# Forget-gate logits in strips over summed halves, and parameter arithmetic one block later, in a hybrid decoder layer

## The chip, the cores and the metric

The kernel runs on one core of a Trainium2 chip. The metric is device time in microseconds (us) from launch to end, as the median of several executions; lower is better. A core has a matrix engine (TensorE, "PE" in the profile, with its weight loads as "PEld"), three elementwise engines (VectorE or "DVE", ScalarE or "ACT", GpSimd or "POOL"), and SyncE ("SP"), which here only starts transfers. Each engine has its own instruction queue and runs it in order. Engines wait for each other on semaphores. SBUF is the on-chip memory; matrix products land in PSUM, in banks of 512 float32 columns.

## The reference

One layer with 256 tokens and model width 4096, everything in float32:

```
u = rmsnorm(h, g_pre);  p = u @ w_in          # 4096 x 12296
fq fk fv fgate f_logit sq sk sv sgate su ssm_gate lx lru_gate = split(p)
log_f  = log_sigmoid(f_logit + b_forget)      # 8 heads, one column of p each
o_fox  = softmax attention over fq, fk, fv, biased by the cumulative sums of log_f
o_sb   = stick-breaking attention over sq, sk, sv
o_ssm  = S5 state space over su: lam_bar = exp(lam*dt), b_bar = (lam_bar-1)/lam * b, scan, then GLU
o_lru  = gated linear recurrence over lx: log_a = 8 * r * log_sigmoid(lambda)
mixed  = concat(each o * silu(its gate)) @ w_out
out    = h + rmsnorm(mixed, g_post)
```

The `f_logit` part of the projection is only 8 columns wide. It stands for 4096 x 8 weights against the 256 tokens. `lam_bar`, `b_bar` and `log_sigmoid(lambda)` are small per-feature arrays that depend on parameters alone.

## The kernel before

**Blocks and chunks.** `w_in` (without the 8 forget columns) is cut into 24 blocks of 512 columns and `w_out` into 8. Blocks 0 to 3 give the sources `su` and `lx`, 4 to 11 queries and keys, 12 to 15 values, 16 to 23 the gates, 24 to 31 the output. A block is 16 chunks (`CH`), each of 2 x 128 rows of the contraction: 512 KB of weights. All chunks go through a ring of four buffers: SyncE loads `w_raw`, ScalarE writes the rounded half `w_hi` (`high`, line 620), VectorE the rest `w_lo` (`low`, line 1000), and TensorE does 12 matmuls of 512 columns (lines 303 to 305): for both groups of 128 tokens and both rows of the chunk u_hi*w_hi, u_hi*w_lo, u_lo*w_hi. `high` and `low` run `LEAD` = 3 chunks ahead of TensorE.

**The order of the work** is written out by hand. Each engine has a loop over the blocks with a loop over the chunks inside, and everything else is hung at a fixed chunk number: `if c == 4: ...`. Block 0 is written out. In it TensorE turns the 32 tiles of x (`turn`, line 354: two tiles, four transposes, in each chunk). ScalarE takes the turned tile as the high half of u (`take_high`, line 661) and VectorE the low half (`take_low`, line 1131), both into `acts[:, k, :]`: 256 columns of high half and 256 of low half. The matmuls of a chunk wait for the halves of their tiles (`u_lo`). ScalarE also squares x for the norm (`square_half`, line 655, in chunks 5, 7, 9 and 11), and the norm's root stands in chunks 12 to 14. After each block its result is turned by eight transposes (`turn_rows`, line 344) in chunk 1 of the next.

**Forget logits.** `wf` holds the 32 x 8 forget columns split in a high and a low part, padded to 128 columns of weights. From chunk 5 of block 0 on three matmuls in each chunk (line 379), 32 in all, multiply them with both halves of u at once, 512 columns, into `main[:, 2, :]`. ScalarE copies the cross part (line 708), VectorE adds it (line 1176), and TensorE waits for that (`fl_dve`) before the turn in block 1. In block 1 `token_logits` (line 388, chunk 3) adds high and low rows by a matmul that also turns the result so that tokens are rows, `forget_values` adds bias and norm, ScalarE and VectorE form the log-sigmoid, `forget_sums` (lines 395 to 397, chunk 9) the cumulative sums.

**Parameter arithmetic.** `s5_angles`, `s5_expm1` and `s5_factors` (10, 11 and 10 small VectorE instructions of 128x32) and `lru_series`, `lru_decays` stand in chunks 4, 9, 10, 5 and 7 of block 0, their exponentials, tangent and sines on ScalarE in chunks 2, 6 and 8. `take_s5(0)` (line 1181) then copies the first group's parameters, `take_source(0)` (line 1185) the first source behind block 3; `s5_inputs` (line 425) waits for the latter in chunk 0 of block 4. `s5_outputs` (line 436) are matmuls with 32-column weights, each into its own 32 partitions of PSUM.

**Loops.** Block 1 is written out; blocks 2 and 3 are the two passes of a loop on each of TensorE, ScalarE and VectorE. GpSimd makes constants at the start and has nothing else to do until block 4.

Of the kernel before, what the change touches and what calls it, by code (L numbers as in the profile page):

```python
# [6 lines left out]
F32 = mybir.dt.float32  # L7
# [6 lines left out]
P = 128  # L14
# [45 lines left out]
def hybrid_trunk(nc, x, par, bt, ct, wfg, wglu, wri, gpost, wall, out):  # L60
    ctx = ExitStack()
    with ctx:
        def sb(name, shape, dt=F32):
            return ctx.enter_context(nc.sbuf_tensor(name, shape, dt))
# [20 lines left out]
        small = sb("small", [P, 147])  # L85
        wf = sb("wf", [P, 2 * NK * FT + P], F32R)
        later = sb("later", [P, 2 * P])
# [21 lines left out]
        wf_raw = scr[:, 0:256].rearrange("p (k n) -> p k n", k=NK)  # L109
        wf_parts = wf[:, 0:2 * NK * FT].rearrange("p (k r n) -> p k r n", k=NK, r=2)  # L110
        fl_sel = small[0:2 * FT, 64:64 + FT]
        s5tmp = scr[:, 256:800].rearrange("p (n f) -> p n f", n=17)
# [6 lines left out]
        s5_y = main[:, 3, 0:T]  # L119
        logits = main[:, 2, :]  # L120
        rows = cross[:, :, :].rearrange("p j t -> p (j t)").rearrange("p (a n) -> p a n", a=TT)
# [35 lines left out]
        ss_base = small[:, 72:74]  # L157
        fl_cross, fl_rows = scr[:, 3584:3840], scr[:, 3840:4096]
        fl_z, fl_e = (small[:, 112 + 16 * n:128 + 16 * n].rearrange("p (a n) -> p a n", a=TT)
# [27 lines left out]
        pa, pd = sem("pa"), sem("pd")  # L187
        wf_hi, wf_lo0, wf_lo = sem("wf_hi"), sem("wf_lo0"), sem("wf_lo")
        fl_mm, fl_act, fl_dve = sem("fl_mm"), sem("fl_act"), sem("fl_dve")
# [28 lines left out]
        MIX_AT, MIX_LATE = (4, 5, 6, 7, 10, 11, 12, 13, 15), 3  # L218
        FL_AT = 5
        SPLIT = [2, 3, 4, 5] + [c + LEAD for c in range(4, CH + 1)]  # L220
# [68 lines left out]
        def _(pe):  # L289
# [78 lines left out]
            for c in range(CH):  # L368
                for k in range(max(KC * c + 2, 4), min(KC * c + 4, NK)):
                    turn(k)  # L370
                if c == 0:
                    first_chunk()
                else:
                    pe.wait_ge(u_lo, KC * (c + 1))
                    chunk_in(0, c)
                if c == FL_AT:
                    pe.wait_ge(wf_lo, 1)
                for k in range(3 * (c - FL_AT), min(3 * (c - FL_AT + 1), NK)) if c >= FL_AT else ():
                    mm = pe.matmul(logits, wf[:, 2 * k * FT:2 * k * FT + P], acts[:, k, :], start=(k == 0),  # L379
                                   stop=(k == NK - 1))  # L380
            mm.then_inc(fl_mm, 1)


            def src_block(i):
                def token_logits():

                    for a in range(TT):
                        mm = pe.matmul(side[:, 2, a * FT:(a + 1) * FT], fl_rows[0:2 * FT, a * P:(a + 1) * P],
                                       fl_sel, start=True, stop=True)
                    mm.then_inc(fl_mm, 1)  # L390

                def forget_sums():

                    pe.wait_ge(lf_ready, 1)
                    pe.matmul(side[0:FT, 1, 0:P], logf[:, 0, :], upto[:, :], start=True, stop=True)
                    pe.matmul(side[0:FT, 1, P:T], logf[:, 0, :], later[:, 0:P], start=True, stop=False)
                    pe.matmul(side[0:FT, 1, P:T], logf[:, 1, :], upto[:, :], start=False,
                              stop=True).then_inc(dec_mm, 1)

                for c in range(CH):  # L400
                    if c == T_AT:
                        if isinstance(i, int):
                            pe.wait_ge(fl_dve, 1)
                        turn_rows(i - 1, i - 1)
                    if c == 3 and isinstance(i, int):
                        token_logits()
                    if c == 9 and isinstance(i, int):
                        forget_sums()
                    chunk_in(i, c)

            src_block(1)
            with pe.Fori(2, B_QK - B_SRC) as i:
                src_block(i)
# [200 lines left out]
        def _(act):  # L614
# [62 lines left out]
            for c in range(CH):  # L677
                for k in range(max(KC * c + 2, 4), min(KC * c + 4, NK)):
                    take_high(k)
                for n in range(SPLIT[c], SPLIT[c + 1]):  # L680
                    high(0, n)
                if c == 2:
                    act.activation(tmp(0), col("log_dt"), ACT.Exp).then_inc(pa, 1)

                    act.activation(log_a[0], col("lam"), ACT.Abs).then_inc(pa, 1)
                    act.wait_ge(pa, 2)
                    act.activation(log_a[0], log_a[0], ACT.Exp, scale=-1.0).then_inc(pa, 1)
                if c == 3:
                    act.wait_ge(wf_in, 16)
                    act.activation(wf_parts[:, :, 0, :], wf_raw, ACT.Copy).then_inc(wf_hi, 1)  # L690
# [5 lines left out]
                if c == 6:  # L696
                    act.wait_ge(pd, 9)
                    act.activation(tmp(4), tmp(1), ACT.Exp).then_inc(pa, 1)
                    act.activation(tmp(5), tmp(1), ACT.Tanh, scale=0.5).then_inc(pa, 1)
                if c == 8:  # L700
                    act.activation(tmp(6), tmp(3), ACT.Sin, scale=TWO_PI).then_inc(pa, 1)
                    act.activation(tmp(7), tmp(3), ACT.Sin, scale=TWO_PI / 2).then_inc(pa, 1)
# [22 lines left out]

            act.wait_ge(wf_lo, 1)
            load_inputs(0)

            def src_block(i):
                for c in range(CH):  # L730
                    high(i, c + LEAD)
                    if c == T_AT + 1:
                        take_turned(i - 1)
                    if c == 5 and isinstance(i, int):
                        act.wait_ge(fl_dve, 3)
# [4 lines left out]
                        act.activation(fl_e, fl_e, ACT.Ln, bias=1.0).then_inc(fl_act, 1)  # L740
                    if c == 10 and isinstance(i, int):
                        act.wait_ge(dec_mm, 1)
# [5 lines left out]

            src_block(1)
            with act.Fori(2, B_QK - B_SRC) as i:  # L750
                src_block(i)
# [242 lines left out]
        def _(dve):  # L994
# [151 lines left out]
            for c in range(CH):  # L1146
                for k in range(max(KC * c + 2, 4), min(KC * c + 4, NK)):
                    take_low(k)
                for n in range(SPLIT[c], SPLIT[c + 1]):
                    low(0, n)  # L1150
                if c == 3:

                    dve.memset(wf[:, 2 * NK * FT:2 * NK * FT + P].bitcast(F32), 0.0).then_inc(wf_lo0, 1)
                    dve.wait_ge(wf_hi, 1)
                    dve.wait_ge(consts, N_CONST)
                    dve.tensor_tensor(fl_sel, ident[0:2 * FT, 0:FT], ident[0:2 * FT, FT:2 * FT],
                                      ALU.add).then_inc(wf_lo0, 1)
                    dve.wait_ge(wf_lo0, 1)
                    dve.tensor_tensor(wf_parts[:, :, 1, :], wf_raw, wf_parts[:, :, 0, :].bitcast(F32),
                                      ALU.subtract).then_inc(wf_lo, 1)  # L1160
                if c == 4:
                    s5_angles()
                if c == 5:
                    lru_series()
                if c == 7:
                    lru_decays()
                if c == 9:
                    s5_expm1()
                if c == 10:
                    s5_factors()  # L1170
# [4 lines left out]
            dve.wait_ge(fl_act, 1)  # L1175
            dve.tensor_tensor(fl_rows[0:2 * FT, :], logits[0:2 * FT, 0:T], fl_cross[0:2 * FT, :],
                              ALU.add).then_inc(fl_dve, 1)

            def take_s5(f):
# [6 lines left out]

            dve.wait_ge(pd, n_pd)
            take_s5(0)

# [15 lines left out]
            def src_block(i):  # L1205
                for c in range(CH):
                    low(i, c + LEAD)
                    if c == 4 and isinstance(i, int):
                        forget_values()
                    if c == 7 and isinstance(i, int):  # L1210
                        log_forgets()

            src_block(1)
            with dve.Fori(2, B_QK - B_SRC) as i:
                src_block(i)
            dve.wait_ge(t_free, FT // JB)
            take_source(0)
# [308 lines left out]
        def _(pool):  # L1526
# [175 lines left out]
```

## Time and profile before

| | |
|---|---|
| median of 3 executions | 1525.13 us (1524.93 to 1525.23) |
| profiled execution: from first to last instruction (span) | 1523.3 us |
| TensorE busy | 1513.9 us (99%) |
| VectorE, ScalarE, GpSimd busy | 940.3, 874.8, 102.7 us |
| granted TensorE clock | 0.999 of full speed |
| read from memory | 287.56 MB, 192 GB/s |

The span is one profiled execution's; the runs' times hold about 1.8 us around it. "Busy" adds up instructions of an engine, with overlaps counted once. The chain of work goes back from the last instruction to what released it each time. Times of a matmul in a list of groups overlap those of its neighbours, and the distance between starts is what one costs in a row. A f32 matmul is two records; one with a 32-column weight is written 128*32.

### The profile page before, as it was taken

What the parts mean: (1) busy time and instruction counts of PE and PEld (TensorE: products, weight loads), DVE (VectorE), ACT (ScalarE), POOL (GpSimd) and SP (SyncE); (2) the same over time, 40 slices, a digit from 0 to 9 for tenths busy, and PEclk for the clock granted to TensorE, in tenths of its full rate; (3) what the DMA queues carried; (4) which work ended last, traced back from release to release, by engine and by line L of the source; (5) the groups of instructions that cost most, each with busy time, mean ns of one, the idle gap of its engine ahead of it and who ended that gap; (6) DMA issues with size and microseconds to landing.
All of it is one profiled execution on the core that took longest, in us unless ns stands there. A gap on an engine that the chain in (4) does not pass through costs nothing.

```text
span 1523.3 us, 21941 instructions
## 1 busy us (share of the span) xinstructions
PE 1513.9 (99%) x7054; PEld 1248.5 (82%) x7054; DVE 940.3 (62%) x1173; ACT 874.8 (57%) x1182; POOL 102.7 (7%) x146
## 2 busy tenths in 40 slices
PE   8999999999999999999999999999999999999998
PEld 7888887888888888888888888888888888888886
DVE  6644468898888896566554555455556544444445
ACT  6644476667776666676764545566666444444443
POOL 0000011221202210000001010000000000000000
PEclk9999999999999999999999999999999999999999
DMA  8566656665666666666666555565556866666675
GB/s 312 152 181 192 184 170 192 191 185 176 187 190 185 199 172 195 181 186 197 186 211 193 173 174 177 153 207 168 163 166 209 294 190 198 193 193 193 192 228 193
DMA packets 86702, 292.39 MB, mean 192 GB/s; under 512 B 9976, under 2 KB 13312, under 8 KB 86528
## 3 DMA queue, kind: packets, MB, share of 16 engines
q1 hardware_dynamic: 78480, 280.27, 61.0%
q10 hardware_dynamic: 8176, 11.54, 2.2%
q8 instruction: 26, 0.43, 0.1%
q14 instruction: 20, 0.16, 0.0%
HBM read 287.56 MB, written 4.20 MB: 192 GB/s over the span
## 4 chain that ended last, share of the span: by engine, by line
PE 97%; DVE 1%; issue 1%; ACT 0%; POOL 0%; ACTq 0%; DVEq 0%; POOLq 0%
PE main L303 30%; PE main L305 29%; PE main L304 29%; PE main L344 1%; PE main L484 1%; PE side L425 1%; PE main L436 1%; PE side L354 1%; PE main L486 0%; PE main L379 0%; PE side L517 0%; PE side L508 0%; PE side L472 0%; DVE w_lo L1000 0%; DVE vals L1258 0%
## 5 line engine op out<-in xcount | busy, mean ns | idle before, releaser
L1000 DVE TENSOR_TENSOR w_lo<-w_raw,w_hi 128x1024 fp32r<-128x1024 f32 x518 | 637.5, 1235 | 547.5 <-ACT w_hi L620 546.7
L620 ACT ACTIVATE w_hi<-w_raw 128x1024 fp32r<-128x1024 f32 x518 | 544.8, 1057 | 532.0 <-PE main L305 502.1
L303 PE MATMUL main<-w_hi,acts 128*128 128x512 f32 x2024 | 796.3, 393 | 0.1
L305 PE MATMUL main<-w_hi,acts 128*128 128x512 f32 x2024 | 788.2, 389 | 0.0
L304 PE MATMUL main<-w_lo,acts 128*128 128x512 f32 x2024 | 787.8, 389 | 0.0
L303 PEld LDWEIGHTS main<-w_hi,acts 128*128 128x128 f32 x2024 | 380.0, 188 | 81.2 <-issue 3.3
L305 PEld LDWEIGHTS main<-w_hi,acts 128*128 128x128 f32 x2024 | 379.9, 188 | 80.2
L304 PEld LDWEIGHTS main<-w_lo,acts 128*128 128x128 f32 x2024 | 380.2, 188 | 77.0
L1557 POOL TENSOR_TENSOR scr<-scr 128x256 f32<-128x256 f32 x32 | 31.1, 971 | 484.2 <-ACT scr L724 484.2
L1258 DVE TENSOR_TENSOR_SCAN vals<-small,vals 128x256 f32<-128x256 f32 x64 | 42.5, 705 | 0.0
L635 ACT ACTIVATE cross<-main,small 128x512 f32<-128x512 f32 x40 | 27.6, 689 | 19.4 <-PE main L305 19.4
L1584 POOL COPY scr<-vals 128x256 f32 (+1 forms) x16 | 12.2, 761 | 332.9 <-PE side L509 332.9
L1251 DVE TENSOR_TENSOR vals<-vals 128x512 f32<-128x512 f32 x32 | 22.3, 696 | 1.1
L1265 DVE TENSOR_TENSOR vals<-vals 128x512 f32<-128x512 f32 x32 | 21.9, 683 | 0.0
L1264 DVE TENSOR_TENSOR vals<-vals 128x512 f32<-128x512 f32 x32 | 21.8, 683 | 0.0
L1247 DVE TENSOR_TENSOR vals<-side,vals 128x512 f32<-128x512 f32 x32 | 21.8, 680 | 0.0
L1248 DVE TENSOR_TENSOR vals<-side,vals 128x512 f32<-128x512 f32 x32 | 21.7, 677 | 0.0
L1131 DVE SCALAR_TENSOR_TENSOR acts<-side,pars,acts 128x256 fp32r<-128x256 f32 x32 | 13.9, 475 | 11.9 <-ACT acts L661 11.8
L344 PE MATMUL main<-ident,cross 128*128 128x128 f32 x160 | 20.7, 272 | 0.0
L1566 POOL TENSOR_TENSOR scr<-scr,small 128x128 f32<-128x128 f32 x32 | 20.6, 673 | 0.0
L1580 POOL COPY scr<-br 128x256 f32 (+1 forms) x16 | 13.0, 815 | 104.4 <-DVE br L1297 103.0
L661 ACT ACTIVATE acts<-side,pars 128x256 fp32r<-128x256 f32 x32 | 13.4, 469 | 11.4 <-PE side L354 11.4
(275 smaller groups left out, 820.4 us busy)
## 6 DMA issues: line engine op xcount, KB each, us to landing
w_raw<-in_wall SPq DMA_DIRECT2D x511, 512.0 KB, 3.6
br<-in_x SPq DMA_DIRECT2D x16, 256.0 KB, 7.5
w_raw<-in_wglu SPq DMA_DIRECT2D x8, 512.0 KB, 4.1
out<-br SPq DMA_DIRECT2D x5, 512.0 KB, 3.7
br<-in_gpost ACTq DMA_DIRECT2D x8, 256.0 KB, 5.5
vals<-in_x ACTq DMA_DIRECT2D x8, 256.0 KB, 5.7
scr<-in_x ACTq DMA_DIRECT2D x8, 256.0 KB, 4.5
scr<-in_bt ACTq DMA_DIRECT2D x32, 32.0 KB, 2.4
```

What stands on the lines that cost most here:

```text
L303: pe.matmul(main[:, bank0 + a, :], u_h, wh, start=(k == 0), stop=False)
L304: pe.matmul(main[:, bank0 + a, :], u_h, wl, start=False, stop=False)
L305: mm = pe.matmul(main[:, bank0 + a, :], u_l, wh, start=False, stop=(k == NK - 1))
L344: tr = pe.transpose(main[:, 2 + j // 2, (j % 2) * T + a * P:(j % 2) * T + (a + 1) * P], rows[:, a, j * P:(j + 1) * P], ident[:, :])
L620: act.activation(w_hi[:, c % RING, :], w_raw[:, c % RING, :], ACT.Copy).then_inc(hi_ready, 1)
L635: act.activation(place(a), main[:, a, :], func, scale=scale[:, a:a + 1]).then_inc(bank_free, 1)
L1000: dve.tensor_tensor(w_lo[:, c % RING, :], w_raw[:, c % RING, :], w_hi[:, c % RING, :].bitcast(F32), ALU.subtract).then_inc(lo_ready, 1)
L1247: dve.tensor_tensor(wide(s5_m1), wide(bu), both(cos), ALU.mult).then_inc(s5_dve, 1)
L1251: dve.tensor_tensor(s5_m1, s5_m1, s5_m2, ALU.add).then_inc(s5_dve, 1)
L1258: dve.tensor_tensor_scan(s5_g[:, r * T:(r + 1) * T], radius, s5_m1[:, r * T:(r + 1) * T], 0.0, ALU.mult, ALU.add).then_inc(s5_dve, 1)
L1265: dve.tensor_tensor(wide(s5_m2), wide(s5_g)[:, ::-1, :], wide(sin), ALU.mult).then_inc(s5_dve, 1)
L1557: pool.tensor_tensor(s5_f, s5_k, s5_a, ALU.subtract).then_inc(s5_frac, 1)
```

## The change

- The split weights `wf` go, and with them the 32 matmuls in block 0, the cross copy on ScalarE and the add on VectorE.
- GpSimd pads the plain f32 forget columns to 32 columns a tile (`wf_pad`, a memset and a copy, after the squares), waits for all halves of u, and adds high and low half of each tile: 16 additions of 128 x 512 into `u_sum`.
- TensorE does `strip_logits` in chunk 2 of block 2: 32 f32 matmuls of 256 columns, tile k into partition strip k mod 4 of `side[:, 3, 0:256]`. ScalarE copies the result; `token_logits` (chunk 4) adds the four strips by a selection matrix over 128 rows. The rest of the forget work follows in block 2, chunks 5 to 11.
- The parameter arithmetic stands in the same chunks of block 1 in place of block 0, on VectorE and ScalarE alike; the diff below shows one line of it for each. `take_s5(0)` stands behind block 3.
- Blocks 2 and 3 are written out in place of the loop.

```diff
-        wf = sb("wf", [P, 2 * NK * FT + P], F32R)
+        wf_pad = scr[:, 1024:2048].rearrange("p (k n) -> p k n", k=NK)
+        fl_sel = small[:, 64:64 + FT]
+        u_sum = [vals[:, :, :].rearrange("p a (k t) -> p (a k) t", t=T), br[:, 32:48, :]]
-        logits = main[:, 2, :]
+        logits = side[:, 3, 0:T]
-        FL_AT = 5
+        PAR_BLOCK = 1
+        FL_AT, FL_BLOCK = (2, 3, 4, 5, 6, 8, 10, 11), 2
...
@@ block.tensor
-                if c == FL_AT:
-                    pe.wait_ge(wf_lo, 1)
-                for k in range(3 * (c - FL_AT), min(3 * (c - FL_AT + 1), NK)) if c >= FL_AT else ():
-                    mm = pe.matmul(logits, wf[:, 2 * k * FT:2 * k * FT + P], acts[:, k, :], start=(k == 0),
-                                   stop=(k == NK - 1))
-            mm.then_inc(fl_mm, 1)
             def src_block(i):
+                def strip_logits():
+
+                    pe.wait_ge(wf_ready, 1)
+                    pe.wait_ge(u_ready, NK // 2)
+                    for m in range(NK // 4):
+                        for j in range(4):
+                            k = 4 * m + j
+                            mm = pe.matmul(logits[32 * j:32 * j + 32, :], wf_pad[:, k, :],
+                                           u_sum[k // 16][:, k % 16, :], start=(m == 0), stop=(m == NK // 4 - 1))
+                    mm.then_inc(fl_mm, 1)
...
                     if c == T_AT:
-                        if isinstance(i, int):
-                            pe.wait_ge(fl_dve, 1)
                         turn_rows(i - 1, i - 1)
-                    if c == 3 and isinstance(i, int):
+                    if c == FL_AT[0] and i == FL_BLOCK:
+                        strip_logits()
+                    if c == FL_AT[2] and i == FL_BLOCK:
                         token_logits()
...
-            src_block(1)
-            with pe.Fori(2, B_QK - B_SRC) as i:
+            for i in range(1, B_QK - B_SRC):
                 src_block(i)
@@ block.scalar
-            act.wait_ge(fl_mm, 1)
-            act.activation(fl_cross[0:2 * FT, :], logits[0:2 * FT, T:2 * T], ACT.Copy).then_inc(fl_act, 1)
+                    if c == 2 and i == PAR_BLOCK:
+                        act.activation(tmp(0), col("log_dt"), ACT.Exp).then_inc(pa, 1)
...
+                    if c == FL_AT[1] and i == FL_BLOCK:
+                        act.wait_ge(fl_mm, 1)
+                        act.activation(fl_rows, logits, ACT.Copy).then_inc(fl_act, 1)
@@ block.vector
-                if c == 4:
-                    s5_angles()
...
-            dve.wait_ge(pd, n_pd)
-            take_s5(0)
+            def strip_sums():
+
+                dve.wait_ge(consts, N_CONST)
+                dve.tensor_reduce(fl_sel, ident[:, :].rearrange("p (j n) -> p n j", j=4)[:, 0:FT, :], AX.X,
+                                  ALU.add).then_inc(fl_dve, 1)
...
+                    if c == 4 and i == PAR_BLOCK:
+                        s5_angles()
...
+            dve.wait_ge(pd, n_pd)
+            take_s5(0)
             dve.wait_ge(t_free, FT // JB)
             take_source(0)
@@ block.gpsimd
+            pool.wait_ge(squared, 2 * TT)
+            pool.wait_ge(wf_in, 16)
+            pool.memset(wf_pad, 0.0).then_inc(wf_zero, 1)
+            pool.wait_ge(wf_zero, 1)
+            pool.tensor_copy(wf_pad[:, :, 0:FT], wf_raw).then_inc(wf_ready, 1)
+            pool.wait_ge(u_lo, NK)
+            for k in range(0, NK, 2):
+                pool.tensor_tensor(u_sum[k // 16][:, k % 16:k % 16 + 2, :], acts[:, k:k + 2, 0:T].bitcast(F32),
+                                   acts[:, k:k + 2, T:2 * T].bitcast(F32), ALU.add).then_inc(u_ready, 1)
```

## Rows read from the trace of the kernel before

**Rows 1.** The page: busy time of the engines, and the last chain by engine.
```profile
PE 1513.9 (99%) x7054; PEld 1248.5 (82%) x7054; DVE 940.3 (62%) x1173; ACT 874.8 (57%) x1182; POOL 102.7 (7%) x146
...
PE 97%; DVE 1%; issue 1%; ACT 0%; POOL 0%; ACTq 0%; DVEq 0%; POOLq 0%
```

**Rows 2.** Waits of TensorE: waiter, releaser, us in total, times, longest.
```profile
PE main L362 <- POOL strict L1539: 3.9, 1, 3.9
```

**Rows 3.** The last chain in order of time, blocks 0 to 3: start, us, what.
```profile
22.00 0.44 PE side L354 x4
...
25.21 0.44 PE side L354 x4
...
28.41 0.69 PE main L379 x3
29.10 0.44 PE side L354 x4
...
33.07 0.44 PE side L354 x4
...
66.91 0.46 PE main L379 x2
70.13 0.88 PE main L344 x8
...
116.29 0.87 PE main L344 x8
160.71 0.88 PE main L344 x8
```

**Rows 4.** TensorE in order of time around the first S5 outputs: start, duration, line.
```profile
248.16 0.39 PE L305 MATMUL main<-w_hi,acts 128*128 128x512 f32 x1
248.48 0.41 PE L436 MATMUL main<-vals,scr 128*32 128x256 f32 x2
...
248.72 0.39 PE L436 MATMUL main<-vals,scr 128*32 128x256 f32 x2
...
249.15 0.39 PE L436 MATMUL main<-vals,scr 128*32 128x256 f32 x2
...
249.48 1.15 PE L425 MATMUL side<-scr 32*128 32x256 f32 x16
```

**Rows 5.** The last chain, block 12: one set of f32 matmuls of 256 columns.
```profile
588.66 0.86 PE side L472 x4
```

**Rows 6.** TensorE in order of time, behind the token logits in block 1.
```profile
76.92 0.50 PE L303 MATMUL main<-w_hi,acts 128*128 128x512 f32 x1
77.25 0.40 PE L304 MATMUL main<-w_lo,acts 128*128 128x512 f32 x1
```

**Rows 7.** The page's costliest groups: count, busy us, mean ns, idle before.
```profile
L1000 DVE TENSOR_TENSOR w_lo<-w_raw,w_hi 128x1024 fp32r<-128x1024 f32 x518 | 637.5, 1235 | 547.5 <-ACT w_hi L620 546.7
L620 ACT ACTIVATE w_hi<-w_raw 128x1024 fp32r<-128x1024 f32 x518 | 544.8, 1057 | 532.0 <-PE main L305 502.1
```

**Rows 8.** VectorE in order of time, end of block 3.
```profile
201.98 0.28 DVE L1185 TENSOR_SCALAR scr<-br 128x256 f32<-128x256 f32 x1
```

**Rows 9.** TensorE in order of time, start of block 4.
```profile
202.36 1.15 PE L425 MATMUL side<-scr 32*128 32x256 f32 x16
```

**Rows 10.** ScalarE in order of time, one heavy step of block 0.
```profile
33.32 0.84 ACT L661 ACTIVATE acts<-side,pars 128x256 fp32r<-128x256 f32 x2 [1.61 <-PE side L354]
...
35.00 1.91 ACT L655 ACTIVATE scr<-br 128x2048 f32<-128x2048 f32 x1
```

**Rows 11.** VectorE in order of time: the last low halves of u.
```profile
61.06 0.88 DVE L1131 SCALAR_TENSOR_TENSOR acts<-side,pars,acts 128x256 fp32r<-128x256 f32 x2 [1.34 <-ACT acts L661]
```

**Rows 12.** Instructions of line 1557 on GpSimd: duration ns min/median/max.
```profile
L1557 POOL TENSOR_TENSOR scr<-scr x32: 739/756/1632, 204.5 to 551.0; 128x256 f32<-128x256 f32 x32
```

**Rows 13.** VectorE's groups by form, 196 to 248 us.
```profile
L1268 DVE TENSOR_TENSOR vals<-vals 128x512 f32<-128x512 f32 x2 | 2.2, 1113 | 0.1
L1268 DVE TENSOR_TENSOR scr<-vals 128x512 f32<-128x512 f32 x2 | 1.4, 692 | 0.1
```

More of the change, by code:

```diff
@@ L109, in hybrid_trunk @@
         wf_raw = scr[:, 0:256].rearrange("p (k n) -> p k n", k=NK)
-        wf_parts = wf[:, 0:2 * NK * FT].rearrange("p (k r n) -> p k r n", k=NK, r=2)
-        fl_sel = small[0:2 * FT, 64:64 + FT]
+        wf_pad = scr[:, 1024:2048].rearrange("p (k n) -> p k n", k=NK)
+        fl_sel = small[:, 64:64 + FT]
+        u_sum = [vals[:, :, :].rearrange("p a (k t) -> p (a k) t", t=T), br[:, 32:48, :]]
         s5tmp = scr[:, 256:800].rearrange("p (n f) -> p n f", n=17)
@@ L157, in hybrid_trunk @@
         ss_base = small[:, 72:74]
-        fl_cross, fl_rows = scr[:, 3584:3840], scr[:, 3840:4096]
+        fl_rows = scr[:, 3840:4096]
         fl_z, fl_e = (small[:, 112 + 16 * n:128 + 16 * n].rearrange("p (a n) -> p a n", a=TT)
@@ L187, in hybrid_trunk @@
         pa, pd = sem("pa"), sem("pd")
-        wf_hi, wf_lo0, wf_lo = sem("wf_hi"), sem("wf_lo0"), sem("wf_lo")
+        wf_zero, wf_ready, u_ready = sem("wf_zero"), sem("wf_ready"), sem("u_ready")
         fl_mm, fl_act, fl_dve = sem("fl_mm"), sem("fl_act"), sem("fl_dve")
@@ L375, in _ @@
                     chunk_in(0, c)
-                if c == FL_AT:
-                    pe.wait_ge(wf_lo, 1)
-                for k in range(3 * (c - FL_AT), min(3 * (c - FL_AT + 1), NK)) if c >= FL_AT else ():
-                    mm = pe.matmul(logits, wf[:, 2 * k * FT:2 * k * FT + P], acts[:, k, :], start=(k == 0),
-                                   stop=(k == NK - 1))
-            mm.then_inc(fl_mm, 1)
-            def src_block(i):
+            def src_block(i):
+                def strip_logits():
[7 more added lines that the diff above has]
+                    mm.then_inc(fl_mm, 1)
                 def token_logits():
+                    pe.wait_ge(fl_act, 1)
+                    pe.wait_ge(fl_dve, 1)
                     for a in range(TT):
-                        mm = pe.matmul(side[:, 2, a * FT:(a + 1) * FT], fl_rows[0:2 * FT, a * P:(a + 1) * P],
+                        mm = pe.matmul(side[:, 2, a * FT:(a + 1) * FT], fl_rows[:, a * P:(a + 1) * P],
                                        fl_sel, start=True, stop=True)
@@ L401, in src_block @@
                     if c == T_AT:
-                        if isinstance(i, int):
-                            pe.wait_ge(fl_dve, 1)
                         turn_rows(i - 1, i - 1)
-                    if c == 3 and isinstance(i, int):
+                    if c == FL_AT[0] and i == FL_BLOCK:
+                        strip_logits()
+                    if c == FL_AT[2] and i == FL_BLOCK:
                         token_logits()
-                    if c == 9 and isinstance(i, int):
+                    if c == FL_AT[6] and i == FL_BLOCK:
                         forget_sums()
                     chunk_in(i, c)
-            src_block(1)
-            with pe.Fori(2, B_QK - B_SRC) as i:
+            for i in range(1, B_QK - B_SRC):
                 src_block(i)
@@ L681, in _ @@
                     high(0, n)
[L682 to L690, printed above, removed]
                 if 4 <= c < 12 and c % 2:
@@ L695, in _ @@
                     act.activation(rs_a[:, 0:TT], ms[:, 0:TT], ACT.Sqrt).then_inc(rms_act, 1)
[L696 to L702, printed above, removed]
                 if c == CH - 1:
@@ L724, in turns @@
                 act.activation(s5_k, s5_k, ACT.Copy, bias=-ROUND).then_inc(s5_ang, 1)
-            act.wait_ge(wf_lo, 1)
+            act.wait_ge(wf_ready, 1)
             load_inputs(0)
@@ L731, in src_block @@
                     high(i, c + LEAD)
+                    if c == 2 and i == PAR_BLOCK:
+                        act.activation(tmp(0), col("log_dt"), ACT.Exp).then_inc(pa, 1)
+                        act.activation(log_a[0], col("lam"), ACT.Abs).then_inc(pa, 1)
+                        act.wait_ge(pa, 2)
+                        act.activation(log_a[0], log_a[0], ACT.Exp, scale=-1.0).then_inc(pa, 1)
+                    if c == 6 and i == PAR_BLOCK:
+                        act.wait_ge(pd, 9)
+                        act.activation(tmp(4), tmp(1), ACT.Exp).then_inc(pa, 1)
+                        act.activation(tmp(5), tmp(1), ACT.Tanh, scale=0.5).then_inc(pa, 1)
+                    if c == 8 and i == PAR_BLOCK:
+                        act.activation(tmp(6), tmp(3), ACT.Sin, scale=TWO_PI).then_inc(pa, 1)
+                        act.activation(tmp(7), tmp(3), ACT.Sin, scale=TWO_PI / 2).then_inc(pa, 1)
                     if c == T_AT + 1:
                         take_turned(i - 1)
-                    if c == 5 and isinstance(i, int):
+                    if c == FL_AT[1] and i == FL_BLOCK:
+                        act.wait_ge(fl_mm, 1)
+                        act.activation(fl_rows, logits, ACT.Copy).then_inc(fl_act, 1)
+                    if c == FL_AT[4] and i == FL_BLOCK:
                         act.wait_ge(fl_dve, 3)
@@ L740, in src_block @@
                         act.activation(fl_e, fl_e, ACT.Ln, bias=1.0).then_inc(fl_act, 1)
-                    if c == 10 and isinstance(i, int):
+                    if c == FL_AT[7] and i == FL_BLOCK:
                         act.wait_ge(dec_mm, 1)
@@ L747, in src_block @@
                         take_rows(i, in_rows, ACT.Copy, rstd)
-            src_block(1)
-            with act.Fori(2, B_QK - B_SRC) as i:
+            for i in range(1, B_QK - B_SRC):
                 src_block(i)
@@ L1150, in _ @@
                     low(0, n)
[L1151 to L1160, printed above, removed]
-                if c == 4:
-                    s5_angles()
[L1163 to L1170, printed above, removed]
                 if c == 12:
@@ L1174, in _ @@
                     norm_root()
-            dve.wait_ge(fl_act, 1)
-            dve.tensor_tensor(fl_rows[0:2 * FT, :], logits[0:2 * FT, 0:T], fl_cross[0:2 * FT, :],
-                              ALU.add).then_inc(fl_dve, 1)
             def take_s5(f):
@@ L1207, in src_block @@
                     low(i, c + LEAD)
-                    if c == 4 and isinstance(i, int):
+                    if c == 4 and i == PAR_BLOCK:
+                        s5_angles()
+                    if c == 5 and i == PAR_BLOCK:
+                        lru_series()
+                    if c == 7 and i == PAR_BLOCK:
+                        lru_decays()
+                    if c == 9 and i == PAR_BLOCK:
+                        s5_expm1()
+                    if c == 10 and i == PAR_BLOCK:
+                        s5_factors()
+                    if c == FL_AT[0] and i == FL_BLOCK:
+                        strip_sums()
+                    if c == FL_AT[3] and i == FL_BLOCK:
                         forget_values()
-                    if c == 7 and isinstance(i, int):
+                    if c == FL_AT[5] and i == FL_BLOCK:
                         log_forgets()
-            src_block(1)
-            with dve.Fori(2, B_QK - B_SRC) as i:
+            for i in range(1, B_QK - B_SRC):
                 src_block(i)
+            dve.wait_ge(pd, n_pd)
+            take_s5(0)
             dve.wait_ge(t_free, FT // JB)
```

## The prediction

> **What bounds the kernel.** I read the page first: TensorE is busy for 1513.9 of 1523.3 us and the chain that ended last lies on it for 97% [rows 1]. The reader is to see that no other engine comes near, so a change is worth what it takes off TensorE's own queue, or what it makes TensorE wait. The list of waits has one wait of TensorE that counts, 3.9 us on the constants at the very start [rows 2], which the change leaves alone. The chain in order of time then gives the price of everything TensorE does, since consecutive starts are real intervals, whereas the "mean ns" of a matmul overlaps its neighbour. In the first block a step without forget logits takes 3.21 us (22.00 to 25.21), the next one, with the first three logit matmuls, 3.89 us (25.21 to 29.10) [rows 3]. The whole difference is the 0.69 us of those three matmuls. So the first block runs at TensorE's pace too, and what is taken out of it shortens it.
>
> The granted clock is 0.999 of the high level (2.4 GHz) over the span and the change has nothing that would idle TensorE for long; I give the clock no term.
>
> **What is removed from TensorE.** The 32 logit matmuls (128x128 weights, 512 columns) stand in eleven places on the chain: ten groups of three at 0.69 or 0.70 us (6.94 us together) and a last pair at 0.46 us [rows 3]. Sum: 7.40 us. The step from 29.10 to 33.07 is 3.97 us, 0.08 us over 3.89 [rows 3]: small waits for the halves of u, in the stretch where VectorE runs the S5 angles and the recurrence's series between its work. With these ops gone from block 0, I count those 0.08 us as gained. Removed: 7.48 us.
>
> **What is added to TensorE.** 32 matmuls with 128x32 weights and 256 columns of plain f32, spread over four column strips. The trace has this shape: S5's output, 8 such matmuls in the code, 16 in the records (two records for each f32 one). They take 1.00 us from 248.48 to 249.48; their starts come in fours, at 248.48, at 248.72, once between and at 249.15, after which the next kind starts at 249.48 [rows 4]. Four strips run at once, about 0.215 us for a set of four, and the rest of the 1.00 us is start and turn to the next kind. That set price is the 0.86 us for four records (0.215 each) of an f32 matmul of 128x256 that runs with no neighbour in another strip [rows 5]. The new train has 64 records, or 16 sets: the 1.00 us for the first four sets and 12 x 0.215 = 2.58 us more, 3.58 us. Scaling the whole 1.00 us by four instead would give 4.00 us; 16 sets alone are 3.44 us. I take 3.58, as starts between sets are what repeats. Around the train stand two changes of kind: the last main matmul ahead of the strips takes 0.32 us instead of 0.23 (248.16 to 248.48) [rows 4], and the first one behind f32 work 0.33 us (76.92 to 77.25) [rows 6], so 0.19 us. Added: 3.77 us, between 3.6 and 4.2.
>
> The logits by token (two f32 matmuls) and the cumulative sums are moved from block 1 to block 2 at the same price. The contraction of the former goes from 16 to 128 rows; its moving side stays at 8 columns, and I take no change (at most 0.2 us for each of the two if 128 rows cost more than 16, one set of an f32 matmul: 0.4 us, kept in the range).
>
> **What is moved off block 0 on ScalarE and VectorE.** The parameter ops go to block 1, where the same `high`/`low` pair has a chunk of 2.76 us to itself (25.65 to 28.41, behind the turn [rows 3]). Each pair is made three chunks ahead; it takes 1.06 and 1.24 us [rows 7], so its reader comes some 6 us after it is ready (8.3 us from its release, less 2.3). The ops, at most 2 us of VectorE in a step, and up to two more table loads on ScalarE, hide there. If that cover were gone they would cost what they hold up, about 1 us. The unrolling of the loop over blocks 2 and 3 gives nothing that I can price: the first chunk of a loop's block follows its predecessor without a gap, and the step past the turn starts on time.
>
> `take_s5(0)`, a 0.1 us copy, now stands on VectorE between the last `low` of the third source block and `take_source(0)`. That copy of the source started at 201.98 and takes 0.28 us [rows 8], and TensorE starts S5's inputs at 202.36 [rows 9]; there is hardly any slack, so up to 0.1 us of wait goes onto TensorE. I take 0.05 us.
>
> **What is added on the other engines, at no cost by this forecast.** In block 0 TensorE's step falls from 3.89 to 3.20 us, so its helpers have less time. ScalarE's heavy steps hold two halves of u, one `high` and a square: from 33.32 its square starts at 35.00 and takes 1.91 us, done at about 37.0, 3.7 us after the start [rows 10]. Over 3.20, but a light step (one pair of halves, one `high`, under 2 us) follows each. After the change the next pair would be asked for at about 36.5 (33.32 + 3.20) and gets ScalarE at 37.0, 0.5 us late. It needs 0.84 us there [rows 10] and half of VectorE's 0.88 [rows 11] more, so it is ready at 38.3; its reader starts one chunk and one turn on, at about 39.6. Roughly 1.3 us of slack is left. The root of the norm in step 12 adds one table load there; I reckon about 1 us remains. The cover is that slack: if it is gone, the steps concerned cost 0.3 to 0.5 us each.
>
> POOL makes 16 additions of 128x512 f32. Nearest row: POOL's 128x256 f32 subtraction, 739 ns at least, 756 median, 1632 at most [rows 12]. Twice these: 1.5 us, up to 3.3 us, for all 16 24 to 52 us. They start when the last half of u is written: at 61.94 before (61.06 + 0.88) [rows 11], minus nine groups of logits and the small waits, 55.6 us. The strip train stands behind the chunk after block 2's turn, which starts at 116.29 [rows 3]: with 0.87 us of turn and 2.76 us of chunk 119.9, less 7.48 us, less the logit work that now stands behind it. That work is 1.7 us: from turn to turn block 1 took 46.16 us (70.13 to 116.29), block 2 without it 44.42 (to 160.71) [rows 3]. So 110.7 us. The window is 55 us, 3.4 us for an addition. By the median it is done half-way.
>
> The Trainium skill (GPSIMD Engine Reference, Elementwise — side-by-side cycle accounting) gives 4497 ns for a 2048-element two-input add; a quarter of it, 1.1 us, would be an estimate for one of ours, 18 us for the 16. The sum would be the same by either.
>
> **Sum.** -7.48 + 3.77 + 0.05 = -3.66 us. The profiled execution's span is 1523.3 us, so it should come to 1519.6; the median of the runs is 1525.13, 1.8 us above the span (what lies around it, which the change doesn't touch): 1521.5 us, 0.24% faster. I take 0.2% (3.05 us, a time under 1522.1) as what this kernel's measurement can tell from no change.
>
> **Rivals.**
> (a) Block 0 keeps part of the time: ScalarE and VectorE become late with u and TensorE waits for halves. For it: the heavy step of 3.7 us against 3.20. Against it: the light steps between, and steps of 3.21 us that held before 28 us, though without squares. Price: 4 squares and the root, 0.3 to 0.5 us each, 1.5 to 2 us; time about 1523.2.
> (b) The strip train costs the flat 4.00 us, the token logits get 0.4 us dearer, and stalls of the fifth block shift by a few tenths: about -2.8 us, 1522.3.
> (c) POOL and VectorE slow each other. The f32 ops of VectorE on two SBUF inputs show it: the same 128x512 subtraction took 1113 ns where POOL worked and 692 where it didn't [rows 13]. By that factor of 1.6 a `low` of 1235 ns [rows 7] becomes 2.0 us. With the parameter ops beside it a step of block 1 asks for up to 4 us from VectorE against 2.76, in two or three steps of the sixteen: 2 to 3 us behind, within 6. It decides only from a `low` of some 2.5 us on; then about 2 us are lost, 1523.5. The Trainium skill (GPSIMD Engine Reference, Key points) states this contention for VectorE instructions with two SBUF inputs; the rows agree.
> (d) The other side: POOL is late for the strips. It decides from 3.4 us for an addition; each 0.1 us above costs 1.6 us. It is slower than before by over 0.2% from 3.9 us, where TensorE waits 8 us at the strip train: 1529. Against it: even twice the longest row stays under the window.
> (e) The strips don't run side by side in a long train: 64 x 0.215 = 13.8 us, net +6.6, 1531.5. The S5 rows speak against it.
>
> **Chances.** Forecast 0.62, (a) 0.13, (b) 0.14, (c) 0.05, (d) 0.04, (e) 0.02. The likeliest case's own range is 1520.7 to 1522.1. The range 1520.5 to 1523.2 reaches to (a) and holds (b). Faster by over 0.2%: nearly all of the forecast and a third of (b), with some room for block 0 paying more: 0.68. Within 0.2%: the rest of (b), (a), (c): 0.26. Slower: (d), (e): 0.06.
>
> **What would show it.** Steps of 3.20 us from 28 us on; the first block's turn at about 62.7 instead of 70.13, 7.4 us earlier; POOL additions of 1.5 to 2.5 us that end before 95 us; one train of 64 records of 3.5 to 4.0 us at about 110 us with no wait ahead; block lengths from block 4 on as before. A wait of TensorE on ScalarE's or VectorE's halves in the first 60 us means (a), one on POOL at 110 us (d). The prediction is wrong if the turn comes later than 64 us, if the train takes more than 4.5 us, or if the fifth block's waits grow.

## The result

The changed kernel takes 1529.27 us (median of 12 runs, 1527.87 to 1529.88) against 1525.17 us (12 runs). The ratio is 1.0024 (95% interval 1.0016 to 1.0032): 4.1 us slower, where 3.7 us faster was forecast. The profiled execution's span is 1526.1 us against 1523.3; with a time of 1528.07 us it is the second fastest of the twelve. In the series below one execution of run 1 and one of the kernel before ran at a granted clock of 0.557 and 0.249 and took 2557.88 and 5885.9 us; no ratio counts them.

The page of the changed kernel, the rows that answer to [rows 1]: busy time of the engines, and the last chain by engine.

```profile
PE 1511.2 (99%) x7086; PEld 1244.2 (82%) x7086; DVE 947.7 (62%) x1170; ACT 875.4 (57%) x1182; POOL 130.6 (9%) x164
...
PE 97%; DMA 1%; DVE 1%; ACT 0%; SPq 0%; issue 0%; ACTq 0%
```

TensorE is busy for 2.7 us less than before and the span is 2.8 us longer. So work went, and waiting came. The waits of TensorE in the changed kernel (it had only the 3.9 us before [rows 2]):

```profile
PE main L304 <- ACT cross L642: 5.1, 1, 5.1
PE main L363 <- POOL strict L1534: 3.9, 1, 3.9
```

One wait of 5.1 us, on ScalarE's eviction (line 642) of block 0's result. The last chain in order of time shows what is behind it (start, us, what):

```profile
54.91 0.96 ACT w_hi L627
55.89 2.02 DVE w_lo L1003
58.02 1.07 DVE small L1110
59.12 1.21 DVE small L1112
60.35 1.20 DVE small L1114
61.58 1.19 DVE small L1116
62.79 1.20 DVE small L1129
64.01 0.70 ACT cross L642
64.85 0.77 PE main L304
65.61 0.43 PE main L305
...
69.38 0.88 PE main L345 x8
...
117.42 3.59 PE side L387 x64
```

Lines 1108 to 1129 are the root of the norm in chunk 14 of block 0: instructions on 128 x 2 numbers that wait for each other. Five of them take 1.1 to 1.2 us each. In the kernel before the same ones took 0.16 or 0.17 us (row of VectorE in order of time, kernel before):

```profile
63.71 0.16 DVE L1107 TENSOR_TENSOR small<-small 128x2 f32<-128x2 f32 x1
```

ScalarE's eviction needs the root, and TensorE needs the evicted bank. What runs beside those instructions is on GpSimd, which began its additions at 55.54 (GpSimd in order of time, changed kernel):

```profile
55.54 11.94 POOL L1552 TENSOR_TENSOR vals<-acts 128x512 f32<-128x512 f32 x8 [5.87 <-DVE acts L1134]
67.43 13.99 POOL L1552 TENSOR_TENSOR br<-acts 128x512 f32<-128x512 f32 x8
```

One of the additions, beside line 1112 (the same view, from 59.10 to 60.20 us alone):

```profile
59.03 1.27 POOL L1552 TENSOR_TENSOR vals<-acts 128x512 f32<-128x512 f32 x1
```

It ends at 60.30 us and line 1112 at 60.32. Each of the five slow instructions ends 0.02 to 0.03 us behind the end of the addition that it met.

And the wait has an aftermath. TensorE's granted clock in stretches around it (from:to us, length, busy us and count, clock, DMA share, GB/s):

```profile
58.00:64.00 6.00, 1.74 (x8) 1.00 0.27 87
64.00:66.00 2.00, 1.15 (x3) 0.69 0.12 36
66.00:68.00 2.00, 2.00 (x7) 0.50 0.88 243
68.00:69.30 1.30, 1.30 (x7) 0.94 0.21 76
```

At 0.50 the clock is at its lower level, 1.2 GHz; TensorE had done nothing from 59.74 to 64.85. Its matmuls start 0.43 us apart in place of 0.23, until about 68.2. The 36 matmuls from 54.01 to the turn at 69.22 take 15.21 us; 36 at the pace of a kernel without the wait take 8.30 (below). So the end of block 0 costs 6.9 us: 5.3 us of wait (from where the next matmul would have started, 59.58; the list's 5.1 counts from the end of the last one) and 1.6 us of lower clock. The forecast -3.66 plus 6.9 is +3.2, and the profiled spans differ by 2.8.

Everything else that was predicted for TensorE holds: steps of 3.20 us from 28 us on, the strip train of 64 records in 3.59 us with no wait ahead, and block lengths close to those before behind it.

### The profile page after: what moved, and what is told of

Read it like the earlier page. It is cut to its first block, busy times and chain, and to the rows that moved or that the text cites. A ratio compares the mean times of both kernels' runs of the same rounds, so it can differ in the third digit from the quotient of the medians.

```text
span 1526.1 us, 21924 instructions
## 1 busy us (share of the span) xinstructions
PE 1511.2 (99%) x7086; PEld 1244.2 (82%) x7086; DVE 947.7 (62%) x1170; ACT 875.4 (57%) x1182; POOL 130.6 (9%) x164
## 4 chain that ended last, share of the span: by engine, by line
PE 97%; DMA 1%; DVE 1%; ACT 0%; SPq 0%; issue 0%; ACTq 0%
PE main L304 30%; PE main L306 30%; PE main L305 30%; PE main L345 1%; DMA w_raw<-in_wall 1%; PE main L491 1%; PE side L432 1%; PE main L443 1%; PE main L493 0%; PE side L524 0%; PE side L515 0%; PE side L479 0%; PE main L597 0%; PE main L596 0%; PE main L595 0%; DVE w_lo L1003 0%
## 5 line engine op out<-in xcount | busy, mean ns | idle before, releaser
L345 PEld LDWEIGHTS main<-ident,cross 128*128 128x128 f32 x160 | 18.4, 140 | 1.6
```

Source lines behind the costliest of these rows:

```text
L345: tr = pe.transpose(main[:, 2 + j // 2, (j % 2) * T + a * P:(j % 2) * T + (a + 1) * P], rows[:, a, j * P:(j + 1) * P], ident[:, :])
```

## The experiments

Each time is the median of its runs (5 to 12; runs 8 and 9 are one execution each), beside runs of the kernel before on the same chip (1525.2 to 1525.5 us).

**1. Additions behind the root.** The changed kernel with one more wait:

```diff
+            pool.wait_ge(rms_dve, 8)
             pool.wait_ge(u_lo, NK)
             for k in range(0, NK, 2):
                 pool.tensor_tensor(u_sum[...], ..., ALU.add).then_inc(u_ready, 1)
```

> The changed kernel with one more wait: POOL starts its 16 additions only when VectorE has finished the root of the norm. Theory (the six small instructions of the root each wait for a POOL addition to end, 1.2 us in place of 0.2, so that the norm, the eviction of block 0 and the next block's first matmuls come 5 us late, and TensorE then runs at the lower clock for a while): no wait of TensorE at the end of block 0, root instructions back at 0.15 to 0.2 us, block 1's turn at about 62.5 us, time 1521.5 (1520.7 to 1522.3). Rival (block 0 is too short for the root whatever POOL does): the wait stays and the time is near 1529.

Measured: 1526.30 us, ratio 1.0007 (0.9998 to 1.0015). The place of the wait is cleared: root instructions at 0.16 us, block 1's turn at 62.9 us. But the time is not 1521.5. A new wait stands in its stead (waits of TensorE in this run):

```profile
PE main L304 <- DVE w_lo L1003: 3.5, 1, 3.5
```

The last chain through it, in order of time:

```profile
76.22 1.20 DVE scr L1022
77.55 1.18 DVE scr L1025
...
83.73 1.18 DVE scr L1035
85.24 1.23 DVE w_lo L1003
86.52 0.51 PE main L304
```

The additions now last until 85 us and lie over the S5 angles, the first chain of small dependent instructions that the change had moved into block 1. In the changed kernel itself they ended at 81.4, one microsecond ahead of it. So my theory of the cause stood and its forecast failed: I hadn't looked at what the later additions would meet. The four links in the middle take 1.21 to 1.23 us each. VectorE in order of time, same run, shows which small instructions pay:

```profile
76.14 1.27 DVE L1022 TENSOR_TENSOR scr<-pars,scr 128x32 f32<-128x32 f32 x1
77.33 0.18 DVE L1023 TENSOR_TENSOR scr<-pars,scr 128x32 f32<-128x32 f32 x1
77.55 1.17 DVE L1025 TENSOR_SCALAR scr<-scr 128x32 f32<-128x32 f32 x1
```

Line 1025 waits for its predecessor's result and pays, and so does each link behind it until GpSimd is done. Line 1023 needs nothing from line 1022, follows it at once and takes 0.18 us. Why it is spared is not shown: line 1022 follows a `low` without a gap too and pays, and in run 2 line 1023 pays as well (below).

The profiled execution of this run is its fastest, with a mean clock of 0.999. Seven of the eleven that the ratio counts have 0.998; whether those had the lower clock behind the wait is open.

**2. Half the grain.** The changed kernel with 32 additions of 128x256 for the 16 of 128x512, at the same place:

```diff
-            for k in range(0, NK, 2):
-                pool.tensor_tensor(u_sum[k // 16][:, k % 16:k % 16 + 2, :], ...
+            for k in range(NK):
+                pool.tensor_tensor(u_sum[k // 16][:, k % 16, :], ...
```

> The changed kernel with 32 additions of 128x256 in place of 16 of 128x512, starting at the same point. Theory, VectorE gets in only between POOL instructions: each small root instruction waits half as long, 0.6 to 0.7 us, the root is 2 to 3 us late in place of 5.2, TensorE waits about 2.5 us, and the clock falls less or not at all: 1523.5 to 1526. Rival, POOL just takes a share of the port's time while it works: root instructions as slow as with the long additions, time near 1529.

Measured: 1525.28 us, ratio 1.0000 (0.9991 to 1.0008). As the theory has it: a link of the root takes 0.65 us (VectorE in order of time),

```profile
58.16 0.65 DVE L1112 TENSOR_TENSOR small<-small 128x2 f32<-128x2 f32 x1
58.85 0.67 DVE L1114 TENSOR_SCALAR small<-small 128x2 f32<-128x2 f32 x1
...
77.28 0.78 DVE L1023 TENSOR_TENSOR scr<-pars,scr 128x32 f32<-128x32 f32 x1
```

TensorE waits 1.9 us for the eviction, and the clock stays at its higher level. Another 1.1 us of wait on `low` comes in block 1, since these additions last into the angles.

**3. The additions alone.** The kernel before, with GpSimd's 16 additions behind its constants and the last half of u. Nothing reads what they write.

> The kernel before with the 16 additions alone put behind its constants and the last half of u; nothing reads their result, all else is as before. Theory: the root's instructions at 63.5 us take 1.2 us each, the eviction of block 0 is some 5 us late, TensorE waits 3 to 4 us in block 1's first chunk and has the lower clock for some chunks after: 1529 to 1531. Rival (the shorter block 0 or the moved parameter arithmetic is the cause): no change, 1525.2.

Measured: 1531.44 us, ratio 1.0041 (1.0028 to 1.0054). One added loop on an idle engine, whose result nobody waits for, costs 6 us. A link of the root (VectorE in order of time), the wait of TensorE and its clock in stretches:

```profile
66.33 1.22 DVE L1111 TENSOR_TENSOR small<-small 128x2 f32<-128x2 f32 x1
```

```profile
PE main L305 <- ACT cross L637: 4.0, 1, 4.0
```

```profile
72.00:74.00 2.00, 1.91 (x6) 0.68 0.48 80
74.00:76.00 2.00, 2.00 (x7) 0.50 0.68 246
```

(A wait of 0.9 us for a half of u, ahead of the additions, is in this profile too. Behind it, from the last pair of logit matmuls to block 1's turn, TensorE takes 9.08 us in place of 3.21, so 5.9 us are the additions'.) The rival, that the shorter block 0 or the moved arithmetic is at fault, falls.

**4. The parameter arithmetic alone.** The kernel before, with `s5_angles` to `s5_factors`, the recurrence's series and ScalarE's part moved to block 1, and `take_s5(0)` behind block 3.

> The kernel before with the parameter arithmetic alone moved to block 1 and the copy of the first S5 parameters behind block 3. Theory: hidden on both sides, 1525.1 (within 0.3 us), the 0.08 us of small waits in block 0 gone and up to 0.1 us more ahead of S5's inputs. Rival (the move itself costs): 1526 or more, with a wait of TensorE on VectorE or ScalarE in block 1.

Measured: 1524.98 us, ratio 0.9997 (0.9989 to 1.0006), no wait of TensorE beyond the constants. By itself the move is worth nothing that can be told, and costs nothing.

**5. Both chains out of the additions' way.** Run 1 with the parameter arithmetic in block 3:

```diff
-        PAR_BLOCK = 1
+        PAR_BLOCK = 3
```

> The kernel of the first run (POOL's additions wait for the norm's root) with the parameter arithmetic in block 3 in place of block 1, behind the additions. Theory (VectorE's chains of small dependent instructions lose 1 us a link whenever POOL adds at the same time, and nothing else costs): no wait of TensorE in blocks 0 to 3, the turn of block 2 at about 107.4 us, time 1521.5 (1521.0 to 1522.3), ratio near 0.9976. Rival (the strips or the unrolled loops cost something of their own): 1523 or more with block lengths as in the first run from block 2 on.

Measured: 1520.97 us, ratio 0.9971 (0.9959 to 0.9982): 4.5 us faster than the kernel before. The strips and the loops written out have no price of their own beyond the forecast. The last matmuls of block 0 take 8.30 us in place of 15.21, the turn of block 1 starts at 62.28, that of block 2 at 106.72, and beside the one on the constants TensorE's list has a single wait, 0.2 us for a half of u at 15.5 us, long before any addition. GpSimd's additions in this run (ns min/median/max):

```profile
L1553 POOL TENSOR_TENSOR vals<-acts x8: 1286/2274/2316, 58.2 to 71.0; 128x512 f32<-128x512 f32 x8
```

1.29 us is an addition that nothing disturbs, 2.3 us is one with a `low` in it. Here it is GpSimd that waits, and nobody waits for GpSimd: all are done by 90 us, the strips start at 110.4.

**6. The arithmetic back in block 0.** As run 5, with the parameter arithmetic where the kernel before has it.

> As the run above, but with the parameter arithmetic back in block 0, where the kernel before has it; additions behind the root. Theory: as fast as the run above, 1521.5, within 0.5 us; the parameter move is then worth nothing by itself. Rival (case (a) of the prediction: with steps of 3.2 us block 0 has no room for parameter arithmetic, squares and halves of u): TensorE waits for halves of u in block 0, 0.5 to 3 us, 1522 to 1524.5.

Measured: 1522.67 us, ratio 0.9981 (0.9972 to 0.9991). The rival was right: TensorE waits for low halves of u where VectorE runs angles and series between them.

```profile
PE main L304 <- DVE acts L1147: 1.1, 2, 0.9
```

In block 0 two turns take 1.48 and 0.78 us in place of 0.35: 1.56 us, nearly the 1.7 us between this run and the last. In the long step of the kernel before, the same chains cost 0.08 us. So the parameter move is worth 1.7 us, but only once the logit matmuls are gone from block 0.

**7. The source's copy first.** Run 5 with `take_source(0)` ahead of `take_s5(0)`.

> The first kernel of this call with the copy of the first source ahead of the copy of the S5 parameters behind block 3. Theory: S5's inputs on TensorE start right behind the last matmul of block 4's predecessor, 0.1 us earlier than in the run it is made from; in the time 0.1 us, which the runs can't tell from nothing: 1521.4.

Measured: 1520.66 us, ratio 0.9967 (0.9955 to 0.9979). The 180 matmuls ahead of S5's inputs take 41.06 us, in run 5 41.14, in the kernel before 41.02. The 0.1 us shows in the profile; the times can't tell it. Its median is the lowest of all, and not to be told from run 5's.

**8. The changed kernel again**, unedited, for a second profile.

> The changed kernel once more, for another profile. Its twelve runs spread from 1527.9 to 1529.9 us, and those above 1529 have a mean granted clock of 0.997 in place of 0.999. Theory: the wait ahead of block 1's second chunk is the same 5.5 us in every run, and what differs is for how long TensorE has the lower clock behind it (3.4 us in the profile at hand): a profile at 0.997 shows 6 to 8 us of it. Rival: a second stretch at the lower clock, or longer waits.

Its profile has a mean clock of 0.997 and a span of 1526.8 us. The wait is the same 5.1 us. The stretches:

```profile
58.00:64.00 6.00, 1.64 (x8) 0.91 0.30 87
64.00:66.00 2.00, 1.24 (x3) 0.50 0.14 44
66.00:68.00 2.00, 2.00 (x6) 0.50 0.88 226
68.00:70.00 2.00, 2.00 (x8) 0.57 0.42 90
```

The lower clock begins within the wait and lasts to about 69.7. Adding up the shares below full clock gives 6.8 us at the lower level (1.1 + 2.0 + 2.0 + 1.7), against 3.4 us in the first profile. About half of the surplus falls into the wait and costs nothing. The rest makes the 36 matmuls 0.76 us longer. That explains part of the spread of the changed kernel's runs. Runs reach a span of 1527.9 us, and where their last microsecond goes is open.

**9. Copies for additions.** The changed kernel with 16 copies of the high half, 128x512; the low half is left out of the forget logits.

```diff
-                pool.tensor_tensor(u_sum[...], high, low, ALU.add).then_inc(u_ready, 1)
+                pool.tensor_copy(u_sum[...], high).then_inc(u_ready, 1)
```

> The changed kernel with each of POOL's 16 additions replaced by a copy of the high half (128x512 in, 128x512 out, one input); the low half is left out of the forget logits. Theory (a small VectorE instruction waits for the end of whatever POOL instruction runs, of any kind): root instructions wait for the length of a copy, 0.5 to 0.8 us by the copies of 128x256 before, the root about 2 us late, TensorE waits 1.5 to 2.5 us, span 1521 to 1523. Rival (only POOL instructions with two inputs hold VectorE up): root instructions at 0.15 to 0.2 us, no wait of TensorE, span near 1519.5.

A single execution: 1522.98 us, span 1521.1. A copy takes 0.61 us, and a link of the root now 0.51 to 0.54:

```profile
58.21 0.52 DVE L1112 TENSOR_TENSOR small<-small 128x2 f32<-128x2 f32 x1
58.77 0.54 DVE L1114 TENSOR_SCALAR small<-small 128x2 f32<-128x2 f32 x1
```

TensorE waits 1.1 us. One input on GpSimd's side is enough to hold VectorE up; its instruction's length is what counts.

**10. Half the grain, behind the root.** Runs 1 and 2 together, arithmetic in block 1.

> Additions behind the root as in the first run, as 32 of 128x256; parameter arithmetic in block 1. Theory (each dependent small instruction waits for one POOL instruction, so half the size is half the delay): the links of the S5 angles take 0.65 us in place of 1.2, VectorE falls about 3 us behind in place of 7, inside what three chunks of lead allow, and TensorE waits 0 to 1 us: 1521.3 to 1522.5. Rival (POOL's total work sets the delay, not its grain): 1526, as in the first run.

Measured: 1526.79 us, ratio 1.0009 (1.0000 to 1.0018). The links did take 0.65 to 0.70 us, as expected, but the time is that of run 1, as the rival had it. TensorE waits 3.6 us. The reason is in VectorE's order of time:

```profile
75.34 0.66 DVE L1027 TENSOR_SCALAR scr<-scr 128x32 f32<-128x32 f32 x1
...
81.85 0.70 DVE L1079 TENSOR_SCALAR scr<-scr 128x8 f32<-128x8 f32 x1
82.59 0.20 DVE L1081 RECIPROCAL scr<-scr 128x8 f32<-128x8 f32 x1
...
84.68 2.69 DVE L1090 SCALAR_TENSOR_TENSOR scr<-scr 128x8 f32<-128x8 f32 x4
```

The additions last to 87 us. With the whole grain the seven dear links of the angles filled that time. With half the grain the chain gets through the angles by 80 us and pays on at the links of the recurrence's series, up to 87. As long as there are links left, VectorE is slow until GpSimd is done. A finer grain helps only a chain that ends before the other engine does, as the root's does.

## Why the prediction was wrong

**The step that failed.** "POOL makes 16 additions ... They start when the last half of u is written", under the heading of what costs nothing. I asked whether the strips would have to wait for GpSimd (they don't) and not what VectorE has to do from 55.5 us on. It is the root of the norm, on which block 0's eviction hangs. With the root's links at 1.2 us the eviction came at 64.0 and TensorE waited 5.3 us. Runs 3 (additions alone: 6 us slower) and 5 (both chains clear: 4.5 us faster) show that this is the cause. (A wait of 0.4 us for a half of u at 25 us stands in the changed kernel's profile too; the last chain leads it back to weights that landed late. Runs 3, 5, 9 and 10 have such a wait of 0.2 to 0.9 us in their first 30 us too, ahead of all additions.)

**Rival (c) had the right engine pair and the wrong price.** From two long instructions [rows 13] I took a factor of 1.6 on length, and applied it to `low`. What the runs show is not a factor but an alternation of whole instructions: a VectorE instruction of 0.16 us beside a GpSimd one of 1.27 us takes 1.2 us, seven times as long. `low` takes 1.2 to 2.3 us beside additions, near the 2.0 that I priced, and in run 5 TensorE never waits for it; the short ones that depend on each other are what to look for. The rule of the Trainium skill that I cited (GPSIMD Engine Reference, Key points: contention with VectorE instructions in a two-port mode or with two SBUF inputs) covers the root's three instructions with two SBUF inputs (lines 1110, 1112 and 1116), and the trace agrees. Those with one input (1114 and 1129) were held up alike, 1.19 us; whether they ran in a two-port mode no run here shows. I read the rule for the large instructions alone.

**The clock.** I gave it no term, as nothing would idle TensorE. Something did, and 1.6 us of the 6.9 are the lower clock (some 0.8 more in run 8).

**Removed from TensorE: right.** Block 1's turn came at 62.28 in run 5 against 69.96 by the same reading before, 7.7 us earlier; 7.48 forecast. Of that 0.24 us is chance of the start: the turns at 25 us already stand at 25.05 and 24.81. From there on it is 44.91 us before and 37.47 in run 5, 7.44 us less.

**Added: right.** The train took 3.59 us, forecast 3.58. The first four sets at their row's price and the others at 0.215 us was the right way to stretch it; strips run side by side in a long train too, so (e) falls (its own net of 6.6 us makes 1531.7, not 1531.5). GpSimd was far from late for it, so (d) falls: an addition that nothing disturbed took 1.3 us, where the doubled row gave 1.5. From block 1's turn to block 3's the added work makes 3.58 us (90.58 before, 94.16 in run 5), against 3.77 forecast. The token logits, which I took as unchanged, need 0.36 us of TensorE in place of 0.54.

**Moved: right in part.** Hidden in block 1 while the additions were over in time, by a microsecond. That cover was an accident of the root's being late, and run 1 took it away. I had priced its loss at about 1 us; it was 3.9 (block 1 from turn to turn: 48.36 us in run 1, 44.44 in run 5).

**Case (a)** had no part in the changed kernel: in run 5 squares and root fit into steps of 3.2 us. But its like is real: with the parameter arithmetic left in block 0 (run 6) such steps have no room, and 1.6 us are lost.

**`take_s5(0)`:** 0.05 us forecast, 0.12 measured in run 5 (41.14 against 41.02 us), 0.04 with the order swapped.

**The sum against run 5.** Forecast -3.66 us, measured -4.5 in the times and -4.3 in the spans. S5's inputs start 4.0 us earlier (198.36 against 202.36), the 0.24 us of the start among them. The other 0.3 us, for which the forecast had no term, are in block 4, where a wait on `low` is gone: from S5's inputs of block 4 to those of block 5 it is 46.76 us, before 47.12. Run 4 has 46.71 us there too, run 6 only 46.98; what brings it about was not tried. So the 0.6 us by which the spans beat the forecast are the start (0.24), the cheaper added work (0.19) and block 4 (0.36), less 0.1 in the other terms.

## What to carry to other kernels

Before giving work to an idle GpSimd, list what VectorE does in the same time, and look for chains of small dependent instructions: each link can cost a whole GpSimd instruction. Order the two by a semaphore, or put the chain elsewhere, and check again what the shifted work then meets. A matmul taken out of a step also takes away the cover of everything that had just fitted into the step.

## What the runs showed of the hardware

- GpSimd and VectorE take turns by whole instructions where they meet. A VectorE link ends with the GpSimd instruction that it met and takes about the length of one: 1.2 us beside 1.27 us additions, 0.65 beside 0.73 us ones, 0.52 beside 0.61 us copies. A GpSimd addition with a `low` in it takes 2.3 us in place of 1.29.
- Links that wait for their predecessor were held up as long as additions ran. For instructions that follow another without a wait no rule comes out: line 1023 took 0.18 us in runs 1 and 10 and 0.78 in run 2, and a `low` right behind the root took 1.2 us where one behind another `low` took 2.3 (changed kernel, 63.89 and 80.20 us).
- It hits VectorE instructions with one SBUF input as well (TENSOR_SCALAR of lines 1114 and 1025, 1.2 us). The reciprocals beside them were not held up (0.20 us at 82.59 in run 10, 0.15 at 57.84 in the changed kernel, each within a GpSimd addition).
- A wait of TensorE of 5.1 us goes with the lower clock, for 3.4 us in one profile and 6.8 in another of the same kernel, and one of 4.0 us (run 3) with 3.4 us of it. Waits of 1.9 us (run 2) and 1.1 us (run 9) left the clock as it was. Between them it is open: 3.5 us left it in the profile of run 1 (1.00 from 86 to 88 us), and 3.6 us lowered it in that of run 10 (0.58 from 88 to 92 us).
- 64 records of f32 matmuls of 256 columns in four column strips take 3.59 us, 0.056 us a record.
